# Moving two square roots of the query and key norms forward in the ScalarE order of a two-block network on one core

## The chip, the cores and the metric

The kernel runs on one core of one Trainium2 chip. The metric is the device time of one execution in microseconds (us); less is better. The engines are TensorE (PE), VectorE (DVE), ScalarE (ACT), GpSimd (POOL) and SyncE (SP), which issues the DMAs here.

## The reference

Two blocks are computed on a sequence of 1024 tokens of width 1024. The first has a layer of Fourier mixing and differential attention and a layer of gated short convolution; the second has a pooling mixer and a convolutional feed-forward. The change lies in the input projections of the first layer. Cut to that:

```python
proj = h @ w_in                                   # 1024 x 3072, and hc @ w_in for 256 context rows
q, k, v = split_qkv(proj, q_norm, k_norm)         # q and k: rms_norm over each 64 channels
q, k = apply_axial_rope(q), apply_axial_rope(k)
lam = exp(sum(lq1 * lk1)) - exp(sum(lq2 * lk2)) + lam_init
o = diff_attention(q, concat(kc, k), concat(vc, v), lam)
fo = fourier_mix(proj[..., F0:Q0])
y = concat(fo, norm(o)) * silu(proj[..., G0:])    # the gate
```

where `rms_norm` is `x * rsqrt(mean(x*x) + eps) * g`. Everything is float32.

## The kernel before

The kernel is written by hand: each engine has its own list of instructions, and semaphores order the lists. It is a chain of stages, with a barrier of all engines between them. The change is in the first stage, `even_projections`, which ends about 328 us into the span of 1829.2 us. What follows that stage is untouched.

**Slices.** The projection is computed with float32 split into a high part (fp32r) and a remainder, and three products for each. The weights come in 48 slices of 128 x 512 (`SLICES`): numbers 0 to 15 for the context rows, then eight each for the units k (16 to 23), v (24 to 31), f (32 to 39, the Fourier input) and q (40 to 47). For each slice SP loads `in_raw` (L379), ACT copies it to `in_hi` (`high_slice`, L129), POOL subtracts to get `in_lo` (L132), and PE runs 24 matmuls (L681), three for each of eight row tiles. The three buffers are rings of four slices (`RING`), so ACT may make slice n only when PE is through with slice n - 4. When a unit's last slice is done, ACT copies its eight PSUM banks to SBUF (`copy_out`, L569), and PE's first slice of the next unit waits for each bank's copy. ACT does this three steps behind: f, ending at slice 39, is copied at step 42, after the high parts of slices 40, 41 and 42.

**Gates.** After the slices PE computes eight gate tiles (`matmul3`, L116). Each needs a weight block of 128 x 1024: loaded by SP (L538), made high by ACT (`g_high`, L129), subtracted by POOL (L132). There are two buffers. `g_high(m + 2)` waits until gate tile m is multiplied, and in ACT's list it stands behind the SiLU of tile m (L658), which SP then writes to `gate_scratch` (L541).

**The norm of k and q.** In DVE's list the norm of k (`norm_and_rotate(0, ...)`) stands behind 32 accumulations for the modulation vectors (L859, L863) and four small operations for lambda. It sums the squares of ten tiles (L879, L881), then signals `qk_summed`. ACT takes the square root of the 80 columns of `stat` in `root` (L557) and signals `qk_rooted`. DVE goes on with the reciprocal (L888), two multiplications over all tiles (L890, L895), and the rotation (L905 to L912). Next come the additions that fold the Fourier input (L937 to L955), then the same norm for q with eight tiles, which first waits until all units are copied. Before the change `root` for k and the exponential for lambda (L651) stand at step 45 (`ROOT_AT`), and `root` for q stands behind the SiLU of gate tile 2 (`ROOT_BEHIND_GATE`).

Of the kernel before, what the change touches and what calls it, by code (L numbers as in the profile page):

```python
# [15 lines left out]
ACT = mybir.ActivationFunctionType  # L16
# [6 lines left out]
KT = D // P  # L23
SEQ = 1024
RT = SEQ // P
# [9 lines left out]
KEYT = KEYS // P  # L35
# [21 lines left out]
def program(nc, a, out):  # L57
    ctx = ExitStack()
    with ctx:
        sems = {}  # L60

        def sem(name):
            if name not in sems:
                sems[name] = nc.alloc_semaphore(name)
            return sems[name]
# [7 lines left out]
        def sb(stack, name, shape, dt=F32):  # L73
            return stack.enter_context(nc.sbuf_tensor(name, shape, dt))
# [53 lines left out]
        def split_high(act, dst, src, done):  # L128
            return act.activation(dst, src, ACT.Copy).then_inc(done, 1)  # L129
# [223 lines left out]
        SLICES = [(unit, k, half) for unit in UNITS for k in range(KT) for half in ("kv" if unit == "ctx" else unit)]  # L353
# [4 lines left out]
        def slice_used(eng, n):  # L358

            unit, k, half = SLICES[n]  # L360
            if k == KT - 1:
                eng.wait_ge(sem("in_tile"), FIRST_TILE[unit] + (CT if (unit, half) == ("ctx", "k") else TILES_OF[unit]))
            else:
                eng.wait_ge(sem("in_used"), sum(SLICES[i][1] < KT - 1 for i in range(n + 1)))
# [17 lines left out]
        def high_slice(act, n):  # L382
            act.wait_ge(sem(f"in_landed{n % RING}"), 16 * (n // RING + 1))
            if n >= RING:
                slice_used(act, n - RING)
            split_high(act, in_hi[:, n % RING, :], in_raw[:, n % RING, :], sem("in_high"))
# [20 lines left out]
        def even_projections():  # L407
            with ExitStack() as st:
# [7 lines left out]
                lam_dot = sb(st, "lam_dot", [P, 2])  # L416
                lam_exp = sb(st, "lam_exp", [P, 2])
# [27 lines left out]
                ctx_rows = a["ctx"].rearrange("b (r p) d -> p (b r) d", p=P)  # L445
                CTX_SLICES = 2 * KT
                REST_FROM, REST_PER_SLICE = 28, 2
                ROOT_AT, ROOT_BEHIND_GATE = 45, 2
                TURN_BANK, ADA_BANK, ROW_BANK = 5, 6, 7
                spread_x, spread_c = pair[2], ps[:, 4, 0:CTX]  # L450

# [6 lines left out]
                N_SLICES = len(SLICES)  # L458

                with nc.Block(name="even_in") as block:  # L460
# [85 lines left out]
                    def _(act):  # L546
                        def g_high(m):
                            act.wait_ge(sem(f"gw_landed{m % 2}"), 16 * (m // 2 + 1))
                            if m >= 2:
                                act.wait_ge(sem("gw_done"), m - 1)  # L550
                            else:
                                slice_used(act, N_SLICES - 3 + 2 * m)
                            split_high(act, g_hi[:, m % 2], g_raw[:, m % 2], sem("gw_high"))

                        def root(n, t):
                            act.wait_ge(sem("qk_summed"), n + 1)
                            act.activation(stat[:, 0:t * 8], stat[:, 0:t * 8], ACT.Sqrt, bias=eps[:, 0:1], scale=1.0 / DH)\  # L557
                               .then_inc(sem("qk_rooted"), 1)

                        def copy_out(unit, first=0, end=None):  # L560
                            for i in range(first, end or TILES_OF[unit]):
                                act.wait_ge(sem("in_tile"), FIRST_TILE[unit] + i + 1)
                                if unit == "ctx":
                                    dst = kv[:, i // CT, i % CT, :]
                                elif unit in "kv":
                                    dst = kv[:, "kv".index(unit), CT + i, :]
                                else:
                                    dst = fq[:, "fq".index(unit), i, :]
                                act.activation(dst, ps[:, i, :], ACT.Copy).then_inc(sem("in_copied"), 1)  # L569
# [66 lines left out]
                        for n in range(CTX_SLICES + RING + 3, N_SLICES + 4):  # L636
                            if n < N_SLICES:
                                high_slice(act, n)
                            if n == N_SLICES:
                                g_high(0)  # L640
                            unit = end_of.get(n - RING + 1)
                            if unit == "v":
                                act.wait_ge(norm_x.s("low"), KT)
                            if unit == "f":

                                act.wait_ge(sem("x_spilled"), 16 * KT)
                            if unit:
                                copy_out(unit)
                            if n == ROOT_AT:
                                act.wait_ge(sem("lam_dots"), 2)  # L650
                                act.activation(lam_exp[:, :], lam_dot[:, :], ACT.Exp).then_inc(sem("lam_exped"), 1)  # L651
                                root(0, KEYT)
                        g_high(1)
                        for m in range(KT):
                            act.wait_ge(sem("gw_done"), m + 1)
                            if m >= 2:
                                act.wait_ge(sem(f"gate_spilled{m % 2}"), 16 * (m // 2))
                            act.activation(gate[:, m % 2, :], pair[m % 4], ACT.Silu).then_inc(sem("gate_ready"), 1)  # L658
                            if m + 2 < KT:
                                g_high(m + 2)  # L660
                            if m == ROOT_BEHIND_GATE:
                                root(1, RT)

                    @block.gpsimd
                    def _(pool):
# [126 lines left out]
                    def _(dve):  # L792
# [166 lines left out]
                        norm_and_rotate(1, q_nat, RT)  # L959

        even_projections()
        end_stage()
        h_stack.close()
# [2680 lines left out]
```

## Time and profile before

| | us |
|---|---|
| median of 3 runs | 1831.22 |
| lowest, highest of 3 | 1827.28, 3571.01 |
| profiled execution | 1831.22 |
| its span in the profile | 1829.2 |
| outside the span | 2.0 |

The profile shows one execution. Times in rows are us from the start of the span unless they are marked ns. A bracket at the end of a row is the idle time of that engine just before it, and which event ended it. The share called PEclk is the TensorE clock that was granted, 1.00 being the higher of its two levels.

### The profile page before, as it was taken

The page shows a single profiled execution, that of the slowest core. Times are in us where ns is not written, and L with a number is a line of the kernel's source. Part 1 is how long each engine was busy: PE and PEld are TensorE (multiplying, and loading weights), DVE is VectorE, ACT ScalarE, POOL GpSimd, SP SyncE. Part 2 cuts the span into 40 slices and gives each one's busy share as a digit, 9 for nine tenths or more (in the row PEclk, how much of TensorE's full clock was granted, in tenths as well). Part 3 has the DMA queues.
Part 4 walks back from the last instruction along what each step waited for, and adds up shares of the span by engine and source line. Part 5 has one row for each costly group of instructions (what it writes and reads, how often), then busy time and mean ns, then how long its engine had stood idle before and what let it go on. Part 6 is the DMA issues. An engine that isn't in the chain of part 4 may idle for free.

```text
span 1829.2 us, 22873 instructions
## 1 busy us (share of the span) xinstructions
PE 1763.5 (96%) x8677; PEld 1476.9 (81%) x8677; DVE 1209.2 (66%) x1358; ACT 798.9 (44%) x1250; POOL 760.3 (42%) x450
## 2 busy tenths in 40 slices
PE   6999999889999899999999999999999999999999
PEld 4788888778888788788888889978888888878887
DVE  3734898558888714955455643597666666689875
ACT  4522232556676524533333522745443444444443
POOL 2323322000001032466666521357999999910000
PEclk8999999889999899999999999999999999999999
DMA  9577122100000461122212431302323222286433
GB/s 360 195 226 234 50 67 79 38 24 1 0 0 1 148 186 58 47 70 70 69 58 81 135 118 47 116 24 81 93 81 92 81 85 80 70 323 243 144 121 121
DMA packets 165385, 188.32 MB, mean 103 GB/s; under 512 B 9454, under 2 KB 117543, under 8 KB 165159
## 3 DMA queue, kind: packets, MB, share of 16 engines
q1 hardware_dynamic: 165287, 187.00, 31.4%
q8 instruction: 64, 1.05, 0.2%
q14 instruction: 34, 0.28, 0.0%
HBM read 152.37 MB, written 34.60 MB: 102 GB/s over the span
## 4 chain that ended last, share of the span: by engine, by line
PE 53%; DVE 4%; ACT 2%; issue 1%; DMA 1%; SPq 0%; ACTq 0%; DVEq 0%
PE ps L3160 20%; PE ps L2168 14%; PE ps L3211 10%; PE ps L2228 5%; PE ps L3511 1%; PE ps L3173 1%; DVE cv_lo_p L132 1%; DVE up_lo_p L132 1%; DMA y_a<-y_scratch 1%; DVE residual L2090 0%; ACT residual L3347 0%; PE ps L3177 0%; DVE residual L3069 0%; ACT cv_hi_p L129 0%; ACT residual L1907 0%
## 5 line engine op out<-in xcount | busy, mean ns | idle before, releaser
L3160 PE MATMUL ps<-up_hi_p,st_hi_p 128*128 128x512 f32 x560 | 218.7, 391 | 2.9 <-ACT residual L2878 2.9
L3160 PE MATMUL ps<-up_lo_p,st_hi_p 128*128 128x512 f32 x560 | 218.6, 390 | 0.0
L3160 PE MATMUL ps<-up_hi_p,st_lo_p 128*128 128x512 f32 x560 | 218.4, 390 | 0.0
L3211 PE MATMUL ps<-down_ring 128*128 128x512 f32 x924 | 210.9, 390 | 2.0 <-DVE down_ring L132 1.8
L3211 PEld LDWEIGHTS ps<-down_ring 128*128 128x128 f32 x924 | 173.1, 188 | 39.6 <-issue 3.9
L132 POOL TENSOR_TENSOR in_lo<-in_raw,in_hi 128x512 fp32r<-128x512 f32 (+1 forms) x54 | 96.5, 1795 | 212.5 <-ACT in_hi L129 212.5
L2168 PE MATMUL ps<-cv_hi_p,cv_st_hi_p 128*128 128x512 f32 x392 | 153.4, 391 | 2.6 <-ACT residual L1886 2.6
L2168 PE MATMUL ps<-cv_lo_p,cv_st_hi_p 128*128 128x512 f32 x392 | 153.2, 391 | 0.0
L2168 PE MATMUL ps<-cv_hi_p,cv_st_lo_p 128*128 128x512 f32 x392 | 153.2, 391 | 0.0
L132 POOL TENSOR_TENSOR st_lo_p<-up_raw,st_hi_p 128x512 fp32r<-128x512 f32 x68 | 100.7, 1485 | 67.7 <-ACT st_hi_p L129 67.7
L2010 DVE TENSOR_TENSOR residual<-ps,residual 128x512 f32<-128x512 f32 x70 | 48.3, 691 | 120.3 <-PE ps L2168 120.3
L3160 PEld LDWEIGHTS ps<-up_hi_p,st_hi_p 128*128 128x128 f32 x560 | 105.5, 188 | 25.1 <-issue 3.3
L3160 PEld LDWEIGHTS ps<-up_hi_p,st_lo_p 128*128 128x128 f32 x560 | 105.6, 189 | 22.0
L3160 PEld LDWEIGHTS ps<-up_lo_p,st_hi_p 128*128 128x128 f32 x560 | 105.6, 189 | 21.9
L3011 DVE TENSOR_TENSOR residual<-ps,residual 128x512 f32<-128x512 f32 x100 | 68.4, 686 | 70.2 <-PE ps L3160 69.9
L1373 ACT ACTIVATE prob<-ps,neg_peak 128x1280 f32<-128x1280 f32 x64 | 84.9, 1326 | 49.8 <-DVE neg_peak L1467 49.7
L1279 PE MATMUL ps<-k_turned,q_turned 128*128 128x512 f32 (+1 forms) x384 | 94.9, 386 | 10.5 <-DVEq L1508 4.1
L1467 DVE TENSOR_REDUCE neg_peak<-ps 128x1 f32<-128x1280 f32 x64 | 95.2, 1487 | 13.7 <-PE ps L1279 13.6
L681 PE MATMUL ps<-in_hi,h_hi 128*128 128x512 f32 x256 | 99.8, 390 | 1.6 <-issue 0.9
L681 PE MATMUL ps<-in_lo,h_hi 128*128 128x512 f32 x256 | 99.6, 389 | 0.0
L681 PE MATMUL ps<-in_hi,h_lo 128*128 128x512 f32 x256 | 99.6, 389 | 0.0
L132 POOL TENSOR_TENSOR cv_st_lo_p<-cv_raw,cv_st_hi_p 128x512 fp32r<-128x512 f32 x50 | 74.6, 1498 | 52.2 <-ACT cv_st_hi_p L129 52.1
(383 smaller groups left out, 4239.4 us busy)
## 6 DMA issues: line engine op xcount, KB each, us to landing
up_raw<-in_ffn_w_in SPq DMA_DIRECT2D x44, 512.0 KB, 5.2
w_raw<-in_ffn_w_out SPq DMA_DIRECT2D x66, 256.0 KB, 2.9
cv_raw<-in_odd_w_in SPq DMA_DIRECT2D x32, 512.0 KB, 5.5
in_raw<-in_even_w_in SPq DMA_DIRECT2D x48, 256.0 KB, 3.8
y_scratch<-residual SPq DMA_DIRECT2D x22, 512.0 KB, 2.6
ada_raw<-in_ada_w SPq DMA_DIRECT2D x16, 512.0 KB, 9.2
square<-in_ada_w SPq DMA_DIRECT2D x16, 512.0 KB, 4.2
rest_odd<-in_ada_w SPq DMA_DIRECT2D x16, 512.0 KB, 4.3
```

The source lines that it names most:

```text
L132: return eng.tensor_tensor(dst, src, high.bitcast(F32), ALU.subtract).then_inc(done, 1)
L681: last = pe.matmul(ps[:, bank, :], x[:, k, r * P:(r + 1) * P], w[:, n % RING, :], start=(k == 0 and x is x_hi and w is in_hi), stop=(k == ...
L1279: last = pe.matmul(score[m][:, b:e], q_turned[:, m, t * P:(t + 1) * P], k_turned[:, m, part, b:e], start=(part == 0), stop=(part == 1))
L1373: act.activation(prob[:, t % 2, m, :], score[m], ACT.Exp, bias=neg_peak[:, t, m:m + 1], accum_out=total[:, t, m:m + 1]).then_inc(sem("expe ...
L1467: dve.tensor_reduce(neg_peak[:, t, m:m + 1], score[m], AX_X, ALU.max, negate=True)\
L2010: dve.tensor_tensor(dst, ps[:, bank(g, p), :], base, ALU.add).then_inc(sem(name), 1)
L2168: last = pe.matmul(out, w[a_], x[b_], start=(first and a_ == 0 and b_ == 0), stop=(stop and a_ == 1), skip_group_check=skip)
L2228: last = pe.matmul(ps[:, 2 * (d % 4) + c, :], w[a_], x[k][:, c * BANK:(c + 1) * BANK], start=(k == 0 and a_ == 0 and x is y_hi), stop=(k = ...
L3011: dve.tensor_tensor(dst, ps[:, bank(j, p), :], base, ALU.add).then_inc(sem(name), 1)
L3160: last = pe.matmul(ps[:, bank(j, p), :], w[p][:, kk * P:(kk + 1) * P], x[p][:, kk, :], start=(first and w is st_hi and x is up_hi), stop=( ...
L3173: pe.matmul(ps[:, plain_bank(j, kind, side), :], part[FIRST_SLOT[j][kind, half]][:, ks], x_hi, start=(kk == 0 and half == 0 and part is st ...
L3211: last = pe.matmul(ps[:, 4 * (i % 2) + m, :], slot[:, s, m * P:(m + 1) * P], slot[:, x, :], start=(k == 0 and s == 0 and x == 2 and DOWN[i ...
```

## The change

ACT's list is reordered; nothing else is. The exponential for lambda and the square root for k move from behind the high part of slice 45 to behind that of slice 39. The square root for q moves from behind gate tile 2's SiLU, to a place ahead of the SiLU of gate tile 0. Two constants go.

```diff
-                ROOT_AT, ROOT_BEHIND_GATE = 45, 2
...
                             if n == N_SLICES:
                                 g_high(0)
+                            if n < N_SLICES and SLICES[n] == ("f", KT - 1, "f"):
+                                act.wait_ge(sem("lam_dots"), 2)
+                                act.activation(lam_exp[:, :], lam_dot[:, :], ACT.Exp).then_inc(sem("lam_exped"), 1)
+                                root(0, KEYT)
                             unit = end_of.get(n - RING + 1)
...
                             if unit:
                                 copy_out(unit)
-                            if n == ROOT_AT:
-                                act.wait_ge(sem("lam_dots"), 2)
-                                act.activation(lam_exp[:, :], lam_dot[:, :], ACT.Exp).then_inc(sem("lam_exped"), 1)
-                                root(0, KEYT)
                         g_high(1)
+                        root(1, RT)
                         for m in range(KT):
...
                             if m + 2 < KT:
                                 g_high(m + 2)
-                            if m == ROOT_BEHIND_GATE:
-                                root(1, RT)
```

ACT's list around the end of unit f and the start of unit q, before the change. The group of 8 `in_hi` ahead of the `fq` copies is slices 35 to 42, and `stat` is the square root for k:

```order
L569 ACTIVATE residual<-ps 128x512 x8
L129 ACTIVATE in_hi<-in_raw 128x512 x8
L569 ACTIVATE fq<-ps 128x512 x8
L129 ACTIVATE in_hi<-in_raw 128x512 x3
L651 ACT_TABLE_LOAD
L651 ACTIVATE lam_exp<-lam_dot 128x2
L557 ACT_TABLE_LOAD
L557 ACTIVATE stat<-stat,eps 128x80
```

The same place after the change:

```order
L568 ACTIVATE residual<-ps 128x512 x8
L129 ACTIVATE in_hi<-in_raw 128x512 x5
L642 ACT_TABLE_LOAD
L642 ACTIVATE lam_exp<-lam_dot 128x2
L556 ACT_TABLE_LOAD
L556 ACTIVATE stat<-stat,eps 128x80
L129 ACTIVATE in_hi<-in_raw 128x512 x3
L568 ACTIVATE fq<-ps 128x512 x8
```

The exponential and the root, which stood behind all eight copies of f and three more slices, now stand ahead of the high parts of slices 40, 41 and 42 and of the copies of f.

ACT's list from the copies of q on, before the change. The `in_hi` rows of 128x1024 are the gate's weight blocks, `gate` rows are SiLUs, and the root of 64 columns is the one for q:

```order
L569 ACTIVATE fq<-ps 128x512 x8
L129 ACTIVATE in_hi<-in_raw 128x1024
L658 ACT_TABLE_LOAD
L658 ACTIVATE gate<-ps 128x1024
L129 ACTIVATE in_hi<-in_raw 128x1024
L658 ACTIVATE gate<-ps 128x1024
L129 ACTIVATE in_hi<-in_raw 128x1024
L658 ACTIVATE gate<-ps 128x1024
L129 ACTIVATE in_hi<-in_raw 128x1024
L557 ACT_TABLE_LOAD
L557 ACTIVATE stat<-stat,eps 128x64
L658 ACT_TABLE_LOAD
```

The same place after the change:

```order
L568 ACTIVATE fq<-ps 128x512 x8
L129 ACTIVATE in_hi<-in_raw 128x1024
L556 ACTIVATE stat<-stat,eps 128x64
L658 ACT_TABLE_LOAD
L658 ACTIVATE gate<-ps 128x1024
L129 ACTIVATE in_hi<-in_raw 128x1024
```

The root for q, which stood behind three SiLUs and the weight blocks 2 to 4, now stands ahead of all of them, and two table loads are gone from this stretch. The lists of PE, DVE, POOL and SP keep their order.

## Rows read from the trace of the kernel before

**Rows 1.** The page, busy time of each engine over the span.

```profile
PE 1763.5 (96%) x8677; PEld 1476.9 (81%) x8677; DVE 1209.2 (66%) x1358; ACT 798.9 (44%) x1250; POOL 760.3 (42%) x450
```

**Rows 2.** Busy time in stretches of the first stage, with the header naming its columns.

```profile
core 0: us, PE busy (x) PEld busy (x) DVE busy (x) ACT busy (x) POOL busy (x), PEclk, DMA share, GB/s
240.00:262.00 22.00, 22.00 (x99) 18.23 (x98) 21.18 (x33) 5.04 (x6) 4.81 (x2) 1.00 0.16 48
```

**Rows 3.** Timeline of ACT, 174 to 211 us: start, duration, what, [idle before <- releaser].

```profile
174.53 0.63 ACT L129 ACTIVATE in_hi<-in_raw 128x512 fp32r<-128x512 f32 x1 [4.81 <-PE ps L681]
...
207.17 0.63 ACT L129 ACTIVATE in_hi<-in_raw 128x512 fp32r<-128x512 f32 x1 [4.81 <-PE ps L681]
207.82 1.28 ACT L651 ACT_TABLE_LOAD   x1
209.11 0.20 ACT L651 ACTIVATE lam_exp<-lam_dot 128x2 f32<-128x2 f32 x1
...
210.63 0.36 ACT L557 ACTIVATE stat<-stat,eps 128x80 f32<-128x80 f32 x1
```

**Rows 4.** Timeline of DVE, 172 to 224 us.

```profile
172.28 1.28 DVE L863 SCALAR_TENSOR_TENSOR rest_sum<-square,cond_col,rest_sum 128x1024 f32<-128x1024 f32 x1 [1.46 <-DMA square<-in_ada_w]
...
186.33 2.15 DVE L863 SCALAR_TENSOR_TENSOR rest_sum<-rest_odd,cond_col,rest_sum 128x1024 f32<-128x1024 f32 x1 [1.31 <-DMA rest_odd<-in_ada_w]
...
203.08 1.20 DVE L879 TENSOR_TENSOR turn<-residual 128x512 f32<-128x512 f32 x1
204.31 0.69 DVE L881 TENSOR_REDUCE stat<-turn 128x8 f32<-128x512 f32 x1
211.02 0.65 DVE L888 RECIPROCAL stat<-stat 128x80 f32<-128x80 f32 x1 [6.02 <-ACT stat L557]
211.71 5.49 DVE L890 TENSOR_TENSOR residual<-residual,stat 128x5120 f32<-128x5120 f32 x1
217.24 6.47 DVE L895 TENSOR_TENSOR residual<-residual,qk_gain 128x5120 f32<-128x5120 f32 x1
```

**Rows 5.** Timeline of POOL, 207 to 225 us.

```profile
207.88 1.29 POOL L132 TENSOR_TENSOR in_lo<-in_raw,in_hi 128x512 fp32r<-128x512 f32 x1 [4.15 <-ACT in_hi L129]
213.32 5.04 POOL L132 TENSOR_TENSOR in_lo<-in_raw,in_hi 128x512 fp32r<-128x512 f32 x1 [4.15 <-ACT in_hi L129]
218.76 6.09 POOL L132 TENSOR_TENSOR in_lo<-in_raw,in_hi 128x512 fp32r<-128x512 f32 x1 [0.41 <-ACT in_hi L129]
```

**Rows 6.** Timeline of ACT, 250 to 328 us.

```profile
250.63 1.03 ACT L658 ACTIVATE gate<-ps 128x1024 f32<-128x1024 f32 x1 [8.03 <-PE ps L116]
...
281.03 0.35 ACT L557 ACTIVATE stat<-stat,eps 128x64 f32<-128x64 f32 x1 [5.37 <-DVE stat L881]
281.39 1.28 ACT L658 ACT_TABLE_LOAD   x1
...
284.19 1.05 ACT L129 ACTIVATE in_hi<-in_raw 128x1024 fp32r<-128x1024 f32 x1
...
326.79 1.02 ACT L658 ACTIVATE gate<-ps 128x1024 f32<-128x1024 f32 x1 [9.85 <-PE ps L116]
```

**Rows 7.** Timeline of DVE, 286 to 317 us.

```profile
286.46 6.50 DVE L895 TENSOR_TENSOR fq<-fq,qk_gain 128x4096 f32<-128x4096 f32 x1
...
316.03 0.42 DVE L912 TENSOR_TENSOR fq<-fq,turn 128x256 f32<-128x256 f32 x1
```

**Rows 8.** Timeline of POOL, the subtraction of 285 us.

```profile
285.32 3.36 POOL L132 TENSOR_TENSOR in_lo<-in_raw,in_hi 128x1024 fp32r<-128x1024 f32 x1 [8.49 <-ACT in_hi L129]
```

**Rows 9.** Busy time and granted clock around a 5.4 us idle of PE.

```profile
619.00:621.00 2.00, 0.00 (x0) 0.00 (x0) 2.00 (x3) 1.86 (x2) 0.00 (x0) 0.50 1.02 395
621.00:623.00 2.00, 1.88 (x5) 1.49 (x6) 2.00 (x3) 0.00 (x0) 0.00 (x0) 0.50 0.96 344
623.00:625.00 2.00, 2.00 (x6) 1.61 (x5) 2.00 (x3) 1.55 (x2) 0.00 (x0) 0.50 0.58 238
625.00:627.00 2.00, 2.00 (x9) 1.58 (x9) 2.00 (x3) 0.71 (x2) 0.00 (x0) 0.95 0.11 23
```

## The prediction

> **What bounds the kernel now.** I read the page first. PE is busy for 96% of the span [rows 1], so what matters of a reordering of ACT is whether PE is made to wait. Then I read the busy time in stretches of the first stage: between 240 and 262 us PE is busy for 22.00 of 22.00 us at the full clock, ACT for 5.04 us [rows 2]. So PE sets the pace here, and ACT has room in time. Its list is what matters: an instruction that waits holds up everything behind it.
>
> The timelines of ACT, DVE and POOL show who waits now. ACT makes the high part of a slice each time PE has finished one: steps 39 and 45 start at 174.53 and 207.17 us, so a slice takes 32.64 / 6 = 5.44 us [rows 3]. DVE's last sum of squares for k ends at 204.31 + 0.69 = 205.00 us [rows 4]. ACT reaches the root at 210.63 us, after it [rows 3], so ACT never waits there. DVE waits 6.02 us for that root [rows 4], and this wait is what the edit shortens. The root for q is different: ACT waits 5.37 us for DVE's sums, until 281.03 us [rows 6]. Gate tile 3 was still being multiplied, so PE lost nothing. DVE ends its list of the stage at 316.03 + 0.42 = 316.45 us [rows 7], while PE's last gate tile ends at 326.8 us [rows 6]. DVE has 10.3 us to spare, and making it earlier by itself buys nothing.
>
> **The first move: the root for k, from step 45 to step 39.** The high part of slice 39 is made at 174.53 us and takes 0.63. ACT then waits for lambda's dot products and loads the tables; that is hidden, for it must then wait for `qk_summed`. In the old trace that comes at 205.00 us. It comes a little sooner now, as POOL has nothing to subtract while ACT waits. Four DVE operations from 186.33 to 203.08 us are longer than their like, because a POOL subtraction ran beside them: the first takes 2.15 us against 1.28, the last 1.20 us against 0.69, and the two between are 0.76 and 0.25 longer [rows 4]. Together they are 2.4 us longer, which go: `qk_summed` at 202.6 us. ACT stands still for some 27 us.
>
> Queued behind it on ACT are the high parts of slices 40, 41, 42 and the copies of f. PE has slices 36 to 39 in stock when step 39 starts, so it runs dry at 174.53 + 4 x 5.44 = 196.3 us. It restarts when f's first bank is copied. That is 202.6, plus 0.3 for the root (0.36 us, partly overlapped [rows 3]), plus three high parts at 0.5 and one bank at 0.7: about 2.6 us, 205.2 us. **Gap one: 8.9 us.** The eight copies then keep just ahead of PE.
>
> **The port between DVE and POOL** decides how good that is. POOL's subtraction takes 1.29 us alone but 5.04 and 6.09 us when it starts inside L890 and L895, and it ends 1.15 us after these [rows 4, 5]. L895 takes 6.47 us against L890's 5.49 on as many elements [rows 4]: it waited for POOL's turn in the same way. So these instructions exclude each other. After the move POOL's subtraction for slice 40 is ready 1.0 us after the sums, and L890 1.1 us after. If POOL is first, gap one is 8.9 us. If DVE is first, slice 40 is low only at 202.6 + 1.1 + 5.5 + 1.15 = 210.4 us and gap one is 14.1 us. I take the first. It will turn out not to matter for the sum.
>
> The Trainium skill, page "SBUF — State Buffer", section "Who interferes with whom", says that a DVE instruction with two SBUF inputs and a GpSimd instruction that reads SBUF exclude each other for a whole instruction, and that issue order decides who waits. By that rule, the trace agrees: 6.09 us where 1.29 is the time alone.
>
> **The second move: the root for q, ahead of gate tile 0.** DVE's reciprocal for k starts 0.4 us behind the sums, as for q (281.00 to about 281.4), so at 203.0 us instead of 211.02: 8.0 us sooner. From there to the sums for q DVE is busy without a break. The way is 281.0 - 211.0 = 70.0 us in the old trace, with seven POOL subtractions in it (two of 512 columns and five of 1024). Each of the first costs DVE about 1.1 us and each of the second about 2.2: L895 for q takes 6.50 us where four fifths of 5.4 is 4.3 [rows 4, 7]. That is 13 us. After the change there are eight of 512 and two of 1024 in that way, again 13 us. So the sums for q end at 281.0 - 8.0 = **273.0 us**. DVE must have all of q copied 14 us before that, at 259; PE's slice 47 ends at 239.8 + 8.9 + 2 for the clock (below) = 250.7 us, or 256 with the long gap one, so it does not wait.
>
> ACT stands at the root from about 252 us to 273.0. Queued behind it are the SiLUs of tiles 0 and 1 and the high parts of weight blocks 2 and 3; behind these wait POOL's subtractions, SP's writes of gate tiles and loads of blocks, and PE. PE has blocks 0 and 1 in stock only. A gate tile takes (326.79 - 250.63) / 7 = 10.88 us [rows 6], so PE is through with tile 1 at 250.7 + 21.8 = 272.5 us. The restart, counted from the sums: root 0.4, table load 1.3, SiLU 1.0 and high part 1.05 with a little overlap [rows 6]: POOL could start at 3.75. DVE has begun L890 at 1.0; for q it takes 4.4 us, so POOL starts at 5.4 and needs 2.25 us more, as it did at 285.32 (3.36 us, ending at 288.68 and 2.2 after L890) [rows 8]. Low part ready at 7.7, PE starts at 273.0 + 7.75 = 280.75 us. **Gap two: about 8 us.** Tile 2 started at 250.63 + 10.88 = 261.5 us before, so PE is 280.75 - 261.5 = **19.3 us** late. Since DVE's list sets this time, gap one is contained in the 19.3 and is not added to it.
>
> Block 3 has time: SP issues its load after the first SiLU, and POOL subtracts it behind L895, some 14.5 us after the sums; PE wants it at 18.6 or later. From tile 2 on all runs as before: six tiles, 65.3 us.
>
> **The clock.** After PE had idled 5.4 us, the granted clock was 0.50 (1.2 GHz) from before work resumed until 625 us, some 4 us of dense matmuls: 5 and 6 records in 2 us where there are 9 or more at 2.4 GHz [rows 9]. Half of 4 us is lost: 2.0 us for each gap. The one behind gap one is hidden in the 19.3; the one behind gap two is added. Bounds 0 (no fall) and 3 us.
>
> **What comes back.** Two of five table loads go (Sqrt before the q root, and a SiLU load behind it): 2 x 1.28 us of ACT, while ACT waits for PE. Worth nothing; 2.6 us if it were on PE's path. The load of SiLU's table, once hidden under tile 3, is now in the restart at 1.3 us and counted.
>
> The Trainium skill, page "ScalarE: Activation LUTs", section "What ACT_TABLE_LOAD costs", puts a further drain of about 1.38 us on each switch. Here a load starts 0.02 us after the copy before it and the exponential 0.01 us after the load (207.82 + 1.28, then 209.11) [rows 3], so no such drain is seen; by the page's figure the estimate would be 1.4 us later.
>
> **Sum**, against the profiled execution of 1831.22 us, which is also the median of the runs shown (span 1829.2 and 2.0 outside it): 19.3 + 2.0 = 21.3 us. What follows the stage stands behind a barrier and moves as a whole: **1852.5 us**, 1.2% more. Its own range is 1847 to 1858: two us either way on the sums for q, the clock's bounds, and the port.
>
> **Rivals.** (a) The port goes to DVE twice. L895 follows L890 by 0.03 us, and if it got in ahead of POOL's waiting subtraction, block 2 would be low 4.3 us later: 1857. Against it: POOL got its turn between L890 and L895 both times [rows 4, 5, 7, 8]. (b) The gaps add up: if DVE's way to the q sums were tied to PE, by a copy it waits for, gap one with its clock comes on top, 10.9 us: 1863. For it speaks only that the wait for q's copies stands in that way; the margin is 3 to 8 us. (c) Gap two is absent, because the sums for q are ready before 264.8 us (272.5 - 7.75). Then gap one alone remains: 8.9 + 2.0, 1842. DVE would have to save 8 us more. (d) Slower by over 2%, 36.6 us: both gaps add up and the port goes against PE in each (5.2 and 4.3 us more): 1831.2 + 21.3 + 10.9 + 9.5 = 1873. (e) Not slower: DVE's lead pays. If PE's stock (four slices, two blocks) outlasted both waits and the DVE tail or ACT's table loads bounded the stage, the time would be 1831.2 - 2.6 = 1828.6. It decides at k's sums before 193.7 us and q's before 264.8; the rows have 202.6 and 273.0, so the change does what it says for DVE and starves PE.
>
> **Chances.** Forecast 80%, (a) 6%, (b) 4%, (c) 5%, (d) 3%, (e) 2%. The range must hold 8 in 10 and takes in (a) and (c): 1841 to 1861. Faster by over 2% (what a measurement of this kernel can tell from no change) 0.01, within 2% 0.95, slower by over 2% 0.04.
>
> **What would show it.** In the new profile: ACT's idle before L556 about 11 to 13 us behind the exponential for k, ended by DVE's reduce, and about 20 us for q; PE idle 8.9 us from 196 us and some 8 us from 272 us, each followed by a stretch at clock 0.50; the q sums near 273 us; POOL's subtraction for block 2 ending 2.2 us behind L890; the stage ending 21 us later, and all later stages unchanged in length. PE without a gap near 272 us would make me wrong toward (c), gate tile 2 starting later than 284 us toward (a) or (b).

## The result, and the profile after

| | us |
|---|---|
| changed kernel, median of 4 runs (lowest, highest) | 1854.74 (1848.65, 1857.03) |
| kernel before, median of 4 runs | 1830.98 |
| ratio, 95% interval | 1.0132 [1.0098, 1.0165] |
| the same comparison repeated (experiment 8) | 1.0117 [1.0097, 1.0136] |
| profiled execution of the changed kernel; its span | 1848.63; 1846.6 |

The run of 3571.01 us of the kernel before was disturbed and is left out of the ratios. The changed kernel is 1.2 to 1.3% slower, 21 to 24 us, where 21.3 us were forecast.

The page hardly shows it. PE's busy time is the same to 3 us, and its share falls from 96% to 95% [rows 1]:

```profile
PE 1760.8 (95%) x8677; PEld 1471.0 (80%) x8677; DVE 1209.7 (66%) x1358; ACT 794.5 (43%) x1248; POOL 761.8 (41%) x450
```

The view of who waited for whom, for PE, shows it at once. Neither of these two lines has a counterpart before:

```profile
PE ps L679 <- ACT fq L568: 9.7, 1, 9.7
...
PE ps L116 <- POOL in_lo L132: 7.7, 1, 7.7
```

The columns are the total, the number of waits and the longest, in us. One wait of 9.7 us is for a copy of f on ACT, one of 7.7 us for the low part of a weight block. These are gap one and gap two. ACT's timeline of the changed kernel gives their origin (it answers to [rows 3, 6]):

```profile
175.13 1.28 ACT L642 ACT_TABLE_LOAD   x1
188.91 0.20 ACT L642 ACTIVATE lam_exp<-lam_dot 128x2 f32<-128x2 f32 x1 [12.50 <-DVE lam_dot L919]
...
203.25 0.36 ACT L556 ACTIVATE stat<-stat,eps 128x80 f32<-128x80 f32 x1 [12.84 <-DVE stat L879]
203.52 1.65 ACT L129 ACTIVATE in_hi<-in_raw 128x512 fp32r<-128x512 f32 x3
205.08 3.98 ACT L568 ACTIVATE fq<-ps 128x512 f32<-128x512 f32 x8
```

Step 39's high part is done at 175.11 us. ACT loads a table and then stands twice, 12.50 us for the dot products and 12.84 us for DVE's sums. Only then come the three high parts and the copies of f. In the gate tiles the pattern repeats:

```profile
252.04 1.05 ACT L129 ACTIVATE in_hi<-in_raw 128x1024 fp32r<-128x1024 f32 x1
273.34 0.35 ACT L556 ACTIVATE stat<-stat,eps 128x64 f32<-128x64 f32 x1 [20.25 <-DVE stat L879]
273.71 1.28 ACT L658 ACT_TABLE_LOAD   x1
275.00 1.02 ACT L658 ACTIVATE gate<-ps 128x1024 f32<-128x1024 f32 x1
275.92 1.05 ACT L129 ACTIVATE in_hi<-in_raw 128x1024 fp32r<-128x1024 f32 x1
...
293.57 1.03 ACT L658 ACTIVATE gate<-ps 128x1024 f32<-128x1024 f32 x1 [11.19 <-PE ps L116]
...
347.97 1.02 ACT L658 ACTIVATE gate<-ps 128x1024 f32<-128x1024 f32 x1 [9.85 <-PE ps L116]
```

ACT waits 20.25 us for the sums for q, which end at 273.31. The first SiLU starts at 275.00 where it had started at 250.63, and the last at 347.97 where it had started at 326.79 [rows 6]: the stage is 21.2 us longer. DVE's timeline shows the gain that was bought with it ([rows 4, 7]):

```profile
202.53 0.69 DVE L879 TENSOR_REDUCE stat<-turn 128x8 f32<-128x512 f32 x1
203.65 0.65 DVE L886 RECIPROCAL stat<-stat 128x80 f32<-128x80 f32 x1 [0.43 <-ACT stat L556]
204.34 6.49 DVE L888 TENSOR_TENSOR residual<-residual,stat 128x5120 f32<-128x5120 f32 x1
210.86 6.46 DVE L893 TENSOR_TENSOR residual<-residual,qk_gain 128x5120 f32<-128x5120 f32 x1
...
272.62 0.69 DVE L879 TENSOR_REDUCE stat<-turn 128x8 f32<-128x512 f32 x1
...
274.31 4.43 DVE L888 TENSOR_TENSOR fq<-fq,stat 128x4096 f32<-128x4096 f32 x1
278.77 6.44 DVE L893 TENSOR_TENSOR fq<-fq,qk_gain 128x4096 f32<-128x4096 f32 x1
...
310.12 0.42 DVE L910 TENSOR_TENSOR fq<-fq,turn 128x256 f32<-128x256 f32 x1
```

DVE waits 0.43 us for the root instead of 6.02, and ends its list at 310.5 us instead of 316.5. Nothing waits for that end. POOL's timeline shows who got the port ([rows 5, 8]):

```profile
204.21 18.57 POOL L132 TENSOR_TENSOR in_lo<-in_raw,in_hi 128x512 fp32r<-128x512 f32 x6 [27.73 <-ACT in_hi L129]
...
277.05 3.89 POOL L132 TENSOR_TENSOR in_lo<-in_raw,in_hi 128x1024 fp32r<-128x1024 f32 x1 [20.95 <-ACT in_hi L129]
```

At 204.21 us POOL is ahead of DVE's long multiplication, which starts at 204.34 and takes 6.49 us instead of 5.49. At 277.05 POOL comes while DVE's multiplication of 4.43 us runs. It needs 3.89 us, and ends 2.2 us after that one. PE's restarts, in its own timeline:

```profile
205.80 0.77 PE L679 MATMUL ps<-in_hi,h_hi 128*128 128x512 f32 x1 [9.66 <-ACT fq L568]
```

```profile
280.99 1.22 PE L116 MATMUL ps<-h_hi,in_hi 128*128 128x512 f32 x2 [7.72 <-POOL in_lo L132]
```

The granted clock around gap two is the last number but two of each row (the columns are those of [rows 2], and it answers to [rows 9]):

```profile
278.00:280.00 2.00, 0.00 (x0) 0.00 (x0) 1.97 (x2) 0.00 (x0) 2.00 (x1) 0.50 0.93 247
280.00:282.00 2.00, 1.01 (x2) 0.83 (x3) 2.00 (x1) 0.68 (x1) 0.93 (x1) 0.50 0.90 337
282.00:284.00 2.00, 2.00 (x6) 1.60 (x5) 2.00 (x1) 0.38 (x1) 1.54 (x1) 0.50 0.88 247
284.00:286.00 2.00, 2.00 (x10) 1.65 (x10) 1.97 (x2) 0.00 (x0) 2.00 (x1) 1.00 0.06 17
```

It is 0.50 when work resumes and 1.00 again from 284 us on. The tile that starts at 280.99 ends at 293.57, so it takes 12.58 us instead of 10.88.

### The profile page after: what moved, and what is told of

It reads as the page before. It is cut to its first block, busy times and chain, and to the rows that moved or that the text cites. A ratio compares the mean times of both kernels' runs of the same rounds, so it can differ in the third digit from the quotient of the medians.

```text
span 1846.6 us, 22871 instructions
## 1 busy us (share of the span) xinstructions
PE 1760.8 (95%) x8677; PEld 1471.0 (80%) x8677; DVE 1209.7 (66%) x1358; ACT 794.5 (43%) x1248; POOL 761.8 (41%) x450
## 4 chain that ended last, share of the span: by engine, by line
PE 52%; DVE 4%; ACT 2%; issue 1%; DMA 1%; SPq 0%; ACTq 0%; DVEq 0%
PE ps L3158 20%; PE ps L2166 14%; PE ps L3209 10%; PE ps L2226 5%; PE ps L3509 1%; PE ps L3171 1%; DVE cv_lo_p L132 1%; DVE up_lo_p L132 1%; DMA y_a<-y_scratch 1%; DVE residual L2088 0%; ACT residual L3345 0%; PE ps L3175 0%; DVE residual L3067 0%; ACT cv_hi_p L129 0%; ACT residual L1905 0%
## 5 line engine op out<-in xcount | busy, mean ns | idle before, releaser
L3158 PEld LDWEIGHTS ps<-up_hi_p,st_lo_p 128*128 128x128 f32 x560 | 105.4, 188 | 21.8
L3028 DVE SCALAR_TENSOR_TENSOR residual<-residual,cols 128x1023 f32<-128x1023 f32 x44 | 72.8, 1653 | 36.4 <-ACT residual L2890 29.7
```

Source lines behind the costliest of these rows:

```text
L3028: dve.scalar_tensor_tensor(out=y[:, 1:SEQ], in0=x[:, 0:SEQ - 1], scalar=col(FFN_TAP1, first + j), in1=y[:, 1:SEQ], op0=ALU.mult, op1=ALU.a ...
L3158: last = pe.matmul(ps[:, bank(j, p), :], w[p][:, kk * P:(kk + 1) * P], x[p][:, kk, :], start=(first and w is st_hi and x is up_hi), stop=( ...
```

## The experiments

Each was timed against the kernel before on the same chip; the ratio is given with its 95% interval. The start of the last SiLU (326.79 us before, 347.97 after) is the better gauge of the stage. The time at which PE reaches step 39 varies by some 3 us between executions (174.5 us before and after, 177.2 in experiment 1, 177.7 in experiment 3). Where PE's own progress sets the end this is taken off (in experiment 2 by way of step 45, on which the root for k waits). DVE's list does not move with it: from step 39 to the root for k it is 26.1 to 28.8 us in the profiles with that root at step 39. A corrected number is therefore good to 1 or 2 us. None leaves out or changes any of the computation, apart from the additional matmuls of experiment 6.

### Experiment 1: the root for k alone

```diff
 # the changed kernel, with root(1, RT) back behind gate tile 2
+                ROOT_AT, ROOT_BEHIND_GATE = 45, 2
...
-                        root(1, RT)
                         for m in range(KT):
...
+                            if m == ROOT_BEHIND_GATE:
+                                root(1, RT)
```

Expected:

> Only the first move: the exponential and the root for k behind step 39, the root for q in its old place behind gate tile 2. My theory (each move makes its own gap, and gap two is set by DVE's way to the q sums): gap one alone, PE idle some 9.7 us at 196 us and 2.0 us lost to the clock, no gap in the gate tiles, last SiLU of the stage at 326.8 + 11.7 = 338.5 us, time 1830 + 12 = 1842 to 1843. Rival 1 (most of the loss comes with the wait at slice 39): last SiLU near 348, time near 1853. Rival 2 (a wait of ACT only costs where it is in the gate tiles): last SiLU at 327.

Measured: ratio 1.0066 [1.0043, 1.0089]. One gap is left, in the same view:

```profile
PE ps L681 <- ACT fq L569: 8.8, 1, 8.8
```

The last SiLU starts at 341.14 us. Step 39 was 2.7 us late, which leaves 338.5 us, as expected: 11.7 us more than before. Of this, 8.8 us is the gap; the rest goes with the clock, which is 0.50 until 5.6 us after the restart. The root for q is reached at 290.02 us, after its sums, and costs nothing in its old place.

### Experiment 2: the root for q alone

```diff
 # the kernel before, with
                         g_high(1)
+                        root(1, RT)
...
-                            if m == ROOT_BEHIND_GATE:
-                                root(1, RT)
```

Expected:

> Only the second move: the root for q ahead of gate tile 0, the root for k in its old place at step 45. My theory: the q sums end at 274.4 us (281.0 less three POOL subtractions of 2.2 us, of blocks 2 to 4, that no longer stand in DVE's way), PE restarts gate tile 2 at 282.2 us instead of 261.5 us, 20.7 us late, and loses 2.0 us to the clock: last SiLU at 349.5 us, one or two us later than with both moves, though only one gap is left, of some 21 us. Time near 1854. Rival (the two gaps add up to the loss of 21.2 us): last SiLU at 326.8 + 21.2 - 11.7 = 336.3 us, time near 1841.

Measured: ratio 1.0138 [1.0114, 1.0161]. PE's wait and ACT's root:

```profile
PE ps L116 <- POOL in_lo L132: 20.6, 1, 20.6
```

```profile
275.94 0.35 ACT L557 ACTIVATE stat<-stat,eps 128x64 f32<-128x64 f32 x1 [33.13 <-DVE stat L880]
```

The one gap is 20.6 us, and the last SiLU starts at 350.66 us, with step 45 1.5 us late: 349.2 us. So the second move alone costs no less than both. The moves cost 11.7 and 22.4 us singly and 21.2 us together. That rules out that the gaps add up, and supports that DVE's way to the sums for q sets the end. From the root for q to the last SiLU it is 74.72 us here and 74.63 us in the changed kernel. What the first gap costs PE is waited out in the second anyway.

### Experiment 3: the root for q one tile later

```diff
 # the changed kernel, with
-                        root(1, RT)
                         for m in range(KT):
...
                             if m + 2 < KT:
                                 g_high(m + 2)
+                            if m == 0:
+                                root(1, RT)
```

Expected:

> Both moves, but the root for q one gate tile later: behind the SiLU of tile 0 and the high part of weight block 2, so that PE has three blocks in stock when ACT stops. My theory: the q sums end at about 275.5 us, PE works on tile 2 from about 273 to 284 us and block 3 is ready by then, so gap two is gone and gap one with its clock is left: last SiLU at 338 to 339 us, time near 1842. Rival (any wait of ACT for the q sums among the first gate tiles costs PE what ACT waits, about 12 us): last SiLU at 348 us or later.

Measured: ratio 1.0073 [1.0049, 1.0098]. ACT still waits, but PE has no wait in the gate tiles:

```profile
276.74 0.35 ACT L556 ACTIVATE stat<-stat,eps 128x64 f32<-128x64 f32 x1 [8.27 <-DVE stat L880]
...
278.40 1.03 ACT L657 ACTIVATE gate<-ps 128x1024 f32<-128x1024 f32 x1
...
286.97 1.03 ACT L657 ACTIVATE gate<-ps 128x1024 f32<-128x1024 f32 x1 [6.59 <-PE ps L116]
```

The third row is the SiLU of tile 2, which waits for PE again. It starts 21.76 us, two tiles of 10.88, after that of tile 0 (265.21 us), so PE lost nothing in between. The last SiLU starts at 341.37 us, with step 39 3.2 us late: 338.2 us, as in experiment 1. A wait of ACT of 8.27 us costs nothing when PE has three blocks in stock. In the changed kernel PE had two, and ACT's wait of 20.25 us made gap two.

### Experiment 4: the root for k at step 42, ahead of the copies of f

```diff
 # the kernel before, with the root for k moved from n == ROOT_AT to here
                             if n == N_SLICES:
                                 g_high(0)
+                            if n == 42:
+                                act.wait_ge(sem("lam_dots"), 2)
+                                act.activation(lam_exp[:, :], lam_dot[:, :], ACT.Exp).then_inc(sem("lam_exped"), 1)
+                                root(0, KEYT)
                             unit = end_of.get(n - RING + 1)
```

Expected:

> Only the first move, but three steps later: the root for k behind the high parts of slices 40, 41 and 42 and still ahead of the copies of f; the root for q in its old place. My theory (PE's first slice of unit q is held by the copy of f's banks, which stand behind the root, not by the ring of slices): PE still runs dry at 196 us and restarts with the first copied bank at about 205.5 us, a gap of 8 to 10 us and 2.0 for the clock: last SiLU at 337 to 339 us, time near 1842. Rival (the ring's stock of high and low parts is what runs out): three more slices, 16 us, are in stock, no gap, last SiLU at 327 us and time 1830.

Measured: ratio 1.0070 [1.0046, 1.0093], and the last SiLU at 338.74 us, with step 42 1.3 us late: 337.4 us. The high and low parts of three more slices stood ready (POOL ends the last of them at 194.53 us), and yet:

```profile
PE ps L681 <- ACT fq L569: 8.0, 1, 8.0
```

```profile
192.17 0.63 ACT L129 ACTIVATE in_hi<-in_raw 128x512 fp32r<-128x512 f32 x1 [4.81 <-PE ps L681]
...
204.51 0.36 ACT L557 ACTIVATE stat<-stat,eps 128x80 f32<-128x80 f32 x1 [8.89 <-DVE stat L881]
204.78 3.99 ACT L569 ACTIVATE fq<-ps 128x512 f32<-128x512 f32 x8
```

The high part of slice 42 is made at 192.17 us, and PE waits 8.0 us all the same, for the copy of f that starts at 204.78. What holds PE in gap one is the copy of the banks that its next unit overwrites, not the ring of slices.

### Experiment 5: both roots earlier than before, where PE has its stock

```diff
 # the kernel before, with
-                ROOT_AT, ROOT_BEHIND_GATE = 45, 2
+                ROOT_AT, ROOT_BEHIND_GATE = 43, 1
```

Expected:

> The kernel before with the root for k two steps earlier (step 43, behind the copies of f) and the root for q one gate tile earlier (behind tile 1 and the high part of block 3). My theory: DVE's reciprocal for k starts at 205.4 us instead of 211.0 us and its list of the stage ends some 4 to 5 us sooner, near 312 us, but PE has its stock at both places and makes no gap, and DVE's end does not set the stage's end: last SiLU at 326.8 us (give or take the jitter of the stage's start), time the same as before within 0.2%, 1828 to 1833. Rival (DVE's lead or the shorter waits of DVE pay when PE isn't starved): stage and time 3 to 5 us shorter, 1826.

Measured: ratio 1.0012 [0.9997, 1.0028], no change.

```profile
203.52 0.37 ACT L557 ACTIVATE stat<-stat,eps 128x80 f32<-128x80 f32 x1 [3.15 <-DVE stat L881]
...
273.24 0.35 ACT L557 ACTIVATE stat<-stat,eps 128x64 f32<-128x64 f32 x1 [8.26 <-DVE stat L881]
...
326.98 1.02 ACT L658 ACTIVATE gate<-ps 128x1024 f32<-128x1024 f32 x1 [9.85 <-PE ps L116]
```

```profile
310.47 0.42 DVE L912 TENSOR_TENSOR fq<-fq,turn 128x256 f32<-128x256 f32 x1
```

DVE's list ends at 310.9 us, 5.6 us sooner than before, and PE has no wait in the slices or the tiles. The last SiLU starts at 326.98 us. This is the test of rival (e): the lead that both moves give DVE is there, and it is worth nothing, since the stage ends with PE. One step, from 42 to 43, behind the copies of f, removes all of gap one.

### Experiment 6: PE kept busy in gap two

```diff
 # the changed kernel, with
                         for m in range(KT):
+                            if m == 2:
+                                pe.wait_ge(sem("in_copied"), N_TILES - 8 + 2 * m + 2)
+                                for _ in range(34):
+                                    pe.matmul(ps[:, 4, :], h_hi[:, 0, 0:P], h_hi[:, 0, 0:BANK], start=True, stop=True)
                             pe.wait_ge(sem("gw_low"), m + 1)
```

Expected:

> The changed kernel, with 34 more matmuls of 128x512 on PE, whose results nobody reads, ahead of its wait for weight block 2: about 7.7 us of work that fills gap two. They change nothing of when block 2 is ready. My theory (the granted clock falls while PE is idle, and gate tile 2 then takes 12.6 us instead of 10.88): the clock stays at 1.00, tile 2 takes 10.9 us from its first matmul to its SiLU, the last SiLU comes 1.7 us sooner, 346.3 us, time 1852 to 1853. Rival (the slow tile 2 has another cause, as its operands' arrival): tile 2 still 12.6 us. If the filling runs over into tile 2's place, the time grows by the overrun.

Measured: ratio 1.0112 [1.0088, 1.0135]. The clock, in the same view as above, and PE's timeline at the start of tile 2:

```profile
280.00:282.00 2.00, 2.00 (x11) 1.65 (x10) 1.97 (x2) 0.00 (x0) 2.00 (x1) 1.00 0.93 237
282.00:284.00 2.00, 2.00 (x11) 1.65 (x10) 2.00 (x1) 0.80 (x1) 0.93 (x1) 1.00 0.92 345
```

```profile
278.77 4.70 PE L782 MATMUL ps<-h_hi 128*128 128x512 f32 x20
283.30 0.62 PE L116 MATMUL ps<-h_hi,in_hi 128*128 128x512 f32 x2
```

The clock stays at 1.00. Tile 2 takes 11.08 us from its first matmul at 283.30 to its SiLU at 294.38, instead of 12.58. From the root for q to the last SiLU it is 73.49 us against 74.63, a gain of 1.1 us; the filling overran block 2's readiness by 0.4 us. So most of the slow tile behind the gap is the clock's doing: 1.5 of its 1.7 us are gone. The last SiLU itself starts at 348.78 us and not at the 346.3 expected, because the root for k started 2.0 us later here than in the changed kernel (205.29 against 203.25) and the whole chain with it. The gain is seen from the root for q only, in one profile; that way is 74.63, 74.72 and 74.81 us in the changed kernel and experiments 2 and 8. The ratios of experiments 6 and 8, 1.0112 and 1.0117, are too close to show it.

### Experiment 7: the low part of block 2 on DVE

```diff
 # the changed kernel: POOL leaves out m == 2, with a semaphore of its own for it, and in norm_and_rotate
                             dve.wait_ge(sem("qk_rooted"), n + 1)
+                            if n == 1:
+                                dve.wait_ge(sem("gw_high"), 3)
+                                split_low(dve, g_lo[:, 0], g_raw[:, 0], g_hi[:, 0], sem("gw_low_vector"))
                             step(dve.reciprocal(stat[:, 0:t * 8], stat[:, 0:t * 8]))
```

Expected:

> The changed kernel, with the subtraction for weight block 2 taken from POOL and put on DVE, behind the root for q and ahead of its reciprocal. My theory (in gap two POOL waits 1.7 us for DVE's multiplication to leave the port they share, then needs 2.2 us, where DVE needs 1.2 us and waits for nobody): block 2 is ready at 276.97 + 1.25 = 278.2 us instead of 280.94 us, gap two is 5.2 us instead of 7.9, PE restarts at 278.3, last SiLU at 345.3 us, time 2.7 us less than the changed kernel. Rival (DVE's own chain, delayed by 4 us, comes to set block 3): last SiLU 348 us or later. Rival 2 (the shorter gap keeps the clock): a further 1.7 us less.

Measured: ratio 1.0099 [1.0069, 1.0128].

```profile
275.70 1.23 DVE L132 TENSOR_TENSOR in_lo<-in_raw,in_hi 128x1024 fp32r<-128x1024 f32 x1 [3.77 <-ACT in_hi L129]
```

```profile
PE ps L116 <- DVE in_lo L132: 5.1, 1, 5.1
```

```profile
276.00:278.00 2.00, 1.02 (x3) 0.83 (x3) 1.97 (x3) 0.51 (x1) 0.00 (x0) 0.52 0.99 266
278.00:280.00 2.00, 2.00 (x6) 1.61 (x5) 2.00 (x1) 0.14 (x1) 0.00 (x0) 0.50 1.05 361
280.00:282.00 2.00, 2.00 (x6) 1.52 (x6) 1.97 (x2) 0.92 (x1) 0.93 (x1) 0.50 1.00 307
282.00:284.00 2.00, 2.00 (x9) 1.59 (x8) 2.00 (x1) 0.00 (x0) 2.00 (x1) 0.77 0.04 12
```

The wait for the port was as priced: PE restarts 5.02 us behind the start of the root (271.96 to 276.98) where it was 7.65 us (273.34 to 280.99), 2.63 us sooner. But the last SiLU comes only 1.2 us sooner, counted from the same root (73.40 against 74.63 us). Tile 2 took 13.98 us, as the clock stayed at 0.50 into the last row, until 5.9 us after the restart; in the changed kernel it was 3.0 us. The clock fell 0.9 us ahead of the restart here (276.1, worked out from the 0.52 of the first row) and 3.8 us ahead of it in the changed kernel (277.2, from a granted clock of 0.79 between 276 and 278 us), and it rose 6.8 us after its fall in both. So 2.6 us less of waiting came back as 1.2 us, and the clock took the rest. This too is one profile, and the ratio's interval overlaps that of the changed kernel.

### Experiment 8: the changed kernel again

Expected:

> The changed kernel once more, for its interval and for a second profile. My theory: the stage carries 21.2 us of the loss and the rest of the program none, so that the 23.8 us between the first medians and the 17.4 us between the two profiles are scatter of the later stages (311.6 to 315.1 us from the Fourier stage to the output projection in six profiles, and some us behind it). From the root for q to the last SiLU 74.6 us as before, give or take 1.5 us for the clock; ratio to the kernel before 1.0116, with an interval that holds 1.0116. Rival (something behind the stage is slower too): ratio of 1.013 or more, and a later stage that is longer in both profiles of the changed kernel than in all the others.

Measured: ratio 1.0117 [1.0097, 1.0136]. The last SiLU starts at 347.45 us, 74.81 us behind the root for q. Its two waits:

```profile
PE ps L116 <- POOL in_lo L132: 7.7, 1, 7.7
PE ps L679 <- ACT fq L568: 7.3, 1, 7.3
```

Gap one is 7.3 us here and was 9.7 us in the first profile, and the stage's end is the same to 0.5 us. That too says that gap one is contained in gap two's end.

Why gap one varies can be read from the six profiles with the root for k at step 39. From the high part of slice 39 to the root it is 28.77 us in the first profile of the changed kernel, 26.45 here, 27.93 in experiment 1, 27.45 in experiment 3, 28.02 in experiment 6 and 26.12 in experiment 7; PE's wait is 19.1 us less in each (9.66, 7.33, 8.80, 8.33, 8.90 and 7.01). So gap one is what DVE's sums need beyond PE's stock. The four of these that also have the root for q ahead of gate tile 0 have 70.0 to 70.1 us between the two roots, whatever gap one is. That is DVE's way to the sums for q, and it does not feel PE's gap.

Over the ten profiles, the way from the first matmul behind the stage to the output projection is 311.6 to 315.9 us, and from there to the last matmul 1177.4 to 1184.7 us. The four profiles with both roots where the change puts them do not stand out (311.9 to 315.9 and 1177.4 to 1184.7), nor the one of before (315.1 and 1180.1). The profiled execution of the changed kernel is 17.4 us longer in span: 21.2 us from the stage, less 3.8 us of this scatter.

## Why the prediction was right

**The path.** The forecast was 1852.5 us, 21.3 us more. The stage became 21.2 us longer, and the repeated median is 1853.22. The closeness is in part luck: in the four profiles with both roots in these places the root for q starts between 271.96 and 275.29 us, as that for k starts between 201.91 and 205.29, and the first comparison had a median of 1854.74. That the loss goes through DVE's sums for q, and gap one does not add to it, was the step on which the sum hung. Experiments 1, 2 and 8 show it: 11.7 and 22.4 us singly, 21.2 together, and 70.0 to 70.1 us from root to root with a gap one of 7.0 to 9.7 us.

**The term sums for k**: 202.6 us forecast, 203.22 measured (DVE's sums began 0.6 us late). None of the four operations is stretched any more: all sums take 0.68 or 0.69 us.

**Gap one**: 8.9 us forecast, 9.8 lost by PE (the last matmul starts at 195.75, the next at 205.80). The first copied bank as the restart was right, by experiment 4. POOL won the port by 0.13 us, the side that I had taken.

**The sums for q**: 273.0 us forecast, 273.31 measured. Counting POOL's subtractions in DVE's way (eight and two against two and five) came out even, as argued: from the reciprocal for k to the end of the sums for q it is 69.66 us (203.65 to 273.31) where it was 69.98 (211.02 to 281.00).

**The restart**: 280.75 forecast, 280.99 measured. All its links came as read from the old rows: root 0.35, table load 1.28, SiLU, high part, the multiplication ahead on the port, 2.2 us of subtraction. Experiment 7 confirms the port's share by taking it away.

**The clock**: 2.0 us forecast, 1.7 measured, 1.8 and 1.9 in experiments 2 and 8 (tile 2 in 12.68 and 12.77 us). The stated bounds of 0 to 3 us were needed: 3.1 us in experiment 7. Two terms are slightly off in opposite directions, 19.3 against 19.5 for the restart and 2.0 against 1.7 for the clock, and they nearly cancel.

**What comes back**: the two table loads that went (1248 instructions on ACT instead of 1250) were worth nothing by the old rows, where ACT waited 8.03 us for PE behind the one and 5.37 us for DVE behind the other; no run has them alone. DVE's lead was worth nothing either, by experiment 5. The Trainium skill, page "ScalarE: Activation LUTs", section "What ACT_TABLE_LOAD costs", adds a drain of about 1.38 us to a switch. After the change a load stands on PE's path, and the trace has no such drain: the load starts 0.02 us after the root, and the SiLU 0.01 us after the load (273.34 + 0.35, 273.71 + 1.28, 275.00).

**The rivals.** (a) POOL got its turn between the two multiplications again; a stretch of 6.44 us on the second shows it. (b) and (d), that the gaps add up, fall with experiment 2. (c), no gap two, was the right picture for one tile later: experiment 3 has it, with 338.2 us. (e) is experiment 5's. Not tried: whether the scatter of the later stages comes from the clock.

## What to carry to other kernels

An in-order engine that makes operands for another must not wait for a third ahead of them: before a wait is moved up, count what stands behind it in the list and how long the stock of the starved engine lasts. Here it was four slices and two blocks, 21.8 us of PE's work each, against 28 us that ACT stood at the root for k and 20 us at that for q (PE had begun on block 0 before ACT reached the second). One gate tile later ACT's wait for q was 8.3 us and free. For k a wait of 8.9 us ahead of the copies of f still cost 8.0 us, and one of 3.2 us one step later, behind them, cost nothing. The stock is the shortest of all things that the starved engine needs, which here was the copy of its old banks and not the ring. And gaps on one path need not add: ask which chain sets the last restart.

## What the runs showed of the hardware

The granted clock's fall costs no fixed amount, and the length of the gap alone does not give it. Behind gap two's 7.7 us PE lost 1.7 us, behind 20.6 us in experiment 2 it lost 1.8, and behind the 5.1 us of experiment 7 it lost 3.1 us (13.98 - 10.88), with the clock at 0.50 at the restart in all three. With matmuls running through the gap it stayed at 1.00. Behind gap one the same spread shows:

```profile
208.00:210.00 2.00, 2.00 (x8) 1.56 (x7) 2.00 (x1) 1.58 (x4) 2.00 (x1) 0.77 0.00 0
```

```profile
212.00:214.00 2.00, 2.00 (x8) 1.57 (x7) 1.97 (x2) 0.00 (x0) 2.00 (x2) 0.69 0.00 0
```

The first row is from the changed kernel: behind a wait of 9.7 us the clock rises about 3.1 us after the restart at 205.80. The second is from experiment 1: behind a wait of 8.8 us it rises about 5.6 us after the restart at 207.63. In experiment 8 it is 3.4 us behind 7.3. So the clock can take back part of what a shorter gap saves, as in experiment 7. That a shorter gap loses more to it as a rule is not shown.

Between DVE and POOL the instruction that had waited went next in the cases shown here, even when the other engine's next one stood 0.03 us behind: POOL's subtraction of 277.05 us got in between the two multiplications of 274.31 and 278.77. The Trainium skill, page "SBUF — State Buffer", section "Who interferes with whom", gives the exclusion for a whole instruction, by issue order. By that rule, the trace agrees: POOL's subtraction of 204.21 us came first, and DVE's first multiplication for k took 6.49 us where it had taken 5.49.
